# Four output blocks side by side on the column tiles of a modulation product, with transposes in place of selecting sums

## The chip, the cores and the metric

The kernel runs on one NeuronCore of one Trainium2 chip. The metric is device time in microseconds (us) of one execution, lower is better. The five engines (PE, the matrix engine; DVE, the vector engine; ACT, the scalar engine; POOL, the general one; SP, which here issues nearly all DMA loads) run their own instruction streams and wait for each other by semaphores.

## The reference, cut to what matters

One decoder layer over 288 token columns: 256 of a prompt, and 8 sample sequences of 4. Everything is float32. A conditioning vector `c`, one for each of the nine sequences, is multiplied by a large weight matrix to give six modulation vectors of width 2048:

```python
mod = (c @ w_ada + b_ada)[:, None, :]                 # c: 9 x 2048, w_ada: 2048 x 12288
sh1, sc1, gt1, sh2, sc2, gt2 = jnp.split(mod, 6, axis=-1)
h = rmsnorm(x, g_norm1) * (1 + sc1) + sh1
proj = h @ w_in                                       # mixer projections and three gates
branches = jnp.einsum('blnw,nwd->blnd', jnp.stack([y_a, y_b, y_c], axis=2), w_br)
merged = jnp.sum(gate * branches, axis=2)
x = x + gt1 * (merged @ w_o)
h2 = rmsnorm(x, g_norm2) * (1 + sc2) + sh2
x = x + gt2 * hier_moe(h2, ...)
```

`w_ada` is 100.7 MB of the 456 MB that the kernel moves. Its 12288 output columns fall into 24 blocks of 512. Blocks 0 to 3 are `sh1`, 4 to 7 `sc1`, 8 to 23 the other four vectors.

## The kernel before, in words

The program is written by hand, engine by engine, with semaphores; the order of the work is the order of the code. It goes through these stages:

1. **Loading stage.** `x` and `c` arrive, PE sums squares for the norm, and then the first 8 blocks of the modulation product (`sh1`, `sc1`) are computed while their 32 MB stream in through the eight 1 MB slots of `ring8`. As soon as the scales and shifts of a quarter of the model width are known, DVE and ACT modulate that quarter of `xa` and split it into a high part `hh` and a low part `hl`, which float32r products need.
2. **Mix stage.** 48 tiles of 128 output columns of `w_in`, each of two halves, each half 8 x 3 products (lines 1155 to 1157: weights high by x high, high by low, low by high). ACT makes the high part of the weights (`split_hi`, line 595), DVE the low part (`split_lo`, line 765), three buffers deep.
3. **Gates stage.** A loop of 16 steps over `ot`. A step has three gate tiles (six halves), three branch halves, and one of the other 16 modulation blocks, whose weights come through two 1 MB buffers `adaw`.
4. **The `w_o` product**, then routing, 16 experts (a loop over 4 groups), and the output.

**How a modulation block is computed.** The stationary operand is a slice of `cT`: 128 rows (one of the 16 slices `kt` of the contraction) by 32 columns, of which 9 are sequences. It fills a quarter of the PE array's columns, so four such products run side by side on the four column tiles, each writing 32 partitions of PSUM bank 6. Before, `ada_chunk` (line 1126) gives the four column tiles four *different slices of the contraction* of the *same* block: bank 6 ends with four partial sums in partitions 0, 32, 64 and 96. So a block is closed by a selecting sum: ACT copies bank 6 to `part` (`save_part`, line 604), and `ada_select` (line 1135) multiplies each 128 columns of `part` by `sel`, a 0/1 matrix of 9 columns used here, which adds the four partial sums and turns the block so that model width lies on partitions. DVE then adds the bias (`save_mod`) and writes `mod`. All this happens once for every block, 24 times.

In the loading stage a block's 4 chunks `j` are used one by one as they land: PE waits for one slot, does 4 products, and increments `ada_used`; SP waits on `ada_used` to load the slot again (line 309), and the first mixer weights `mixw` (line 315), which lie over the same slots, wait on it too. The blocks come in the order 0, 4, 1, 5, 2, 6, 3, 7, so that each pair completes one quarter `q`. DVE does for each `q`: two `save_mod`, `scales` (line 797), `modulate` (lines 765, 811), a wait for ACT's `hh`, and `hl`. ACT does for each `q`: two `save_part`, its half of `modulate` (line 610), and `hh` (line 623). Only after the fourth quarter do they split the first mixer weights.

In the gates stage PE does the block's chunks 0 and 1 after the first gate tile and 2 and 3 after the third, and `ada_select` after the second branch half.

## Time and profile before

| what | value |
|---|---|
| device time, median of 3 runs | 1684.76 us (1684.45 to 1692.87) |
| profiled execution: span from first to last instruction | 1679.3 us |
| profiled execution: its own device time | not given apart; the fastest run is 5.15 us above the span |
| PE busy | 1587.3 us, 95% of the span |
| DVE, ACT, POOL busy | 41%, 29%, 14% |
| granted PE clock, mean | 0.967 of full |
| DMA | 456.46 MB, 272 GB/s mean |

The profile is one execution on the chip. A line number names a line of the kernel; a helper's line (765 is DVE's `tt`) stands for all its callers, so DVE rows are told apart by the tiles. A float32 product of the modulation, of the selecting sums or of a transpose shows as two MATMUL records, a float32r product (lines 1155 to 1157) as one. A matmul's printed duration includes its way through the pipeline, so the pace of a stream is read from the distances between starts.

### The profile page before, as it was taken

The numbers are of one execution on the slowest core, as the hardware profiler recorded it, in microseconds if no ns is written. First come the engines' busy times: TensorE is split into PE (matmuls) and PEld (weight loads), VectorE is DVE, ScalarE is ACT, GpSimd is POOL, SyncE is SP. The second block draws the span as 40 slices with busy tenths as digits, with TensorE's granted clock in tenths as the row PEclk, the third lists the DMA queues.
The fourth block names the chain that finished last, engine by engine and source line by source line (L and its number), as shares of the span: only waits on it lengthen the run. The fifth ranks groups of instructions, "written<-read, shape, count | busy, mean of one in ns | idle before, by whom it ended". The sixth has DMA issues, their size and how long they took to land.

```text
span 1679.3 us, 27852 instructions
## 1 busy us (share of the span) xinstructions
PE 1587.3 (95%) x10634; PEld 1199.8 (71%) x10634; DVE 686.4 (41%) x1368; ACT 482.7 (29%) x613; POOL 235.2 (14%) x368
## 2 busy tenths in 40 slices
PE   5779999999999999999999989969999999999995
PEld 2169999999899898989898989945345345345342
DVE  2134444434434333434343345572342443443446
ACT  2133333334334433443344333240101101101102
POOL 0017678603200000000000002220000000000002
PEclk9689999999999999999999999977999999999996
DMA  9994545441565676567666765243998998998991
GB/s 379 422 370 165 178 161 177 158 171 58 209 277 236 252 295 273 241 245 298 271 247 240 299 267 175 78 173 135 410 421 361 407 422 361 411 422 356 409 384 56
DMA packets 63102, 456.46 MB, mean 272 GB/s; under 512 B 7728, under 2 KB 8112, under 8 KB 9440
## 3 DMA queue, kind: packets, MB, share of 16 engines
q1 hardware_dynamic: 62352, 454.66, 68.3%
q0 software_dynamic: 720, 1.41, 0.2%
q8 instruction: 17, 0.28, 0.1%
q14 instruction: 13, 0.11, 0.0%
HBM read 452.93 MB, written 3.12 MB: 272 GB/s over the span
## 4 chain that ended last, share of the span: by engine, by line
PE 89%; DMA 5%; DVE 4%; ACT 1%; issue 1%; SPq 0%; POOL 0%; DVEq 0%; ACTq 0%
PE bank L1155 18%; PE bank L1156 17%; PE bank L1157 17%; PE bank L1357 13%; PE bank L1395 7%; DMA ring<-in_w_ada 5%; PE bank L1126 4%; PE bank L1328 3%; PE bank L1313 2%; PE bank L1330 1%; PE bank L1379 1%; PE bank L1135 1%; PE bank L1385 1%; PE bank L1413 1%; PE bank L1345 0%
## 5 line engine op out<-in xcount | busy, mean ns | idle before, releaser
L765 DVE TENSOR_TENSOR wl<-mixw,wh 128x1024 fp32r<-128x1024 f32 x224 | 288.4, 1289 | 460.8 <-ACT wh L595 454.1
L1155 PE MATMUL bank<-hh,wh 128*128 128x288 f32 x1536 | 458.1, 298 | 8.1 <-DVE wl L765 6.7
L1156 PE MATMUL bank<-hl,wh 128*128 128x288 f32 x1536 | 454.3, 296 | 0.0
L1157 PE MATMUL bank<-hh,wl 128*128 128x288 f32 x1536 | 452.6, 295 | 0.0
L595 ACT ACTIVATE wh<-mixw 128x1024 fp32r<-128x1024 f32 x224 | 236.8, 1058 | 345.9 <-PE bank L1157 340.9
L1155 PEld LDWEIGHTS bank<-hh,wh 128*128 128x128 f32 x1536 | 288.8, 188 | 21.8 <-issue 14.9
L1157 PEld LDWEIGHTS bank<-hh,wl 128*128 128x128 f32 x1536 | 290.1, 189 | 0.0
L1156 PEld LDWEIGHTS bank<-hl,wh 128*128 128x128 f32 x1536 | 289.2, 188 | 0.1
L1359 PE MATMUL bank<-ring,xg 128*64 128x512 f32 x512 | 232.0, 600 | 0.0
L1357 PE MATMUL bank<-ring,xg 128*64 128x512 f32 x512 | 232.0, 600 | 0.0
L1357 PEld LDWEIGHTS bank<-ring,xg 128*64 128x64 f32 x512 | 67.3, 138 | 132.1 <-issue 131.6
L1395 PE MATMUL bank<-dring,hid 128*64 128x512 f32 x512 | 113.4, 595 | 13.3 <-DVE hid L765 13.3
L1039 DVE SCALAR_TENSOR_TENSOR x<-bank,mod,x 128x256 f32<-128x256 f32 x272 | 118.1, 477 | 0.0
L1155 PE MATMUL bank<-ysp,wh 128*128 128x288 f32 x384 | 116.4, 303 | 0.0
L1156 PE MATMUL bank<-ysp,wh 128*128 128x288 f32 x384 | 113.1, 294 | 0.0
L1157 PE MATMUL bank<-ysp,wl 128*128 128x288 f32 x384 | 112.7, 293 | 0.0
L765 DVE TENSOR_TENSOR wl<-brw,wh 128x1024 fp32r<-128x1024 f32 x48 | 58.8, 1225 | 99.4 <-ACT wh L595 99.4
L765 DVE TENSOR_TENSOR scaled<-bank,mod 128x32 f32<-128x32 f32 x272 | 38.9, 185 | 144.8 <-PE bank L1313 144.8
L1395 PEld LDWEIGHTS bank<-dring,hid 128*64 128x64 f32 x512 | 35.3, 137 | 81.0 <-issue 64.0
L1155 PE MATMUL bank<-mh,wh 128*128 128x288 f32 x256 | 77.2, 302 | 5.3 <-DVE ml L765 5.3
L1155 PEld LDWEIGHTS bank<-ysp,wh 128*128 128x128 f32 x384 | 72.1, 188 | 13.4 <-issue 13.4
L576 POOL TENSOR_TENSOR sq<-sq 128x288 f32<-128x288 f32 x8 | 6.6, 827 | 533.1 <-ACT sq L753 533.1
(229 smaller groups left out, 1938.3 us busy)
## 6 DMA issues: line engine op xcount, KB each, us to landing
adaw<-in_w_ada SPq DMA_DIRECT2D x64, 1024.0 KB, 5.9
ring<-in_w_gate SPq DMA_DIRECT2D x64, 1024.0 KB, 10.9
ring<-in_w_up SPq DMA_DIRECT2D x64, 1024.0 KB, 12.8
dring<-in_w_down SPq DMA_DIRECT2D x64, 1024.0 KB, 12.8
mixw<-in_w_mix SPq DMA_DIRECT2D x48, 1024.0 KB, 5.0
mixw<-in_w_gt SPq DMA_DIRECT2D x48, 1024.0 KB, 8.5
ring<-in_w_ada SPq DMA_DIRECT2D x32, 1024.0 KB, 17.8
brw<-in_w_br SPq DMA_DIRECT2D x16, 1536.0 KB, 9.4
```

Source lines behind the costliest of these rows:

```text
L595: act.activation(wh[:, b], src, ACT.Copy).then_inc(hi_ready, 1)
L765: return dve.tensor_tensor(out, a, b, op)
L1039: dve.scalar_tensor_tensor(x1[:, f, 0:TP], bank[b + h][:, 0:TP], mod[:, GT2 + f, 0:1], x1[:, f, 0:TP], ALU.mult, ALU.add)
L1126: last = mm(bank[6][32 * q:32 * q + 32, :], cT[:, 4 * j + q, :], buf[:, q, :], start=j == 0, stop=j == ADA_CHUNKS - 1, tile_position=(0, 3 ...
L1155: mm(out, wh[:, s, k, :], hi[:, first + k, :], start=start and k == 0, stop=False)
L1156: mm(out, wh[:, s, k, :], lo[:, first + k, :], start=False, stop=False)
L1157: last = mm(out, wl[:, s, k, :], hi[:, first + k, :], start=False, stop=stop and k == HALF - 1)
L1313: last = mm(bank[b + h][:, 0:T], y[rows, P * j:P * j + P], sT[e_before % 2][rows, :], start=part_ == 0, stop=part_ == 1, tile_position=(64 ...
L1328: mm(bank[b][:, 256 * d:256 * d + 256], thi[0:n, t_, f0:f0 + P], oh[0:n, t_, :], start=t_ == 0, stop=False)
L1357: a = mm(bank[0][0:CAP, :], xg[:, kt, slots], gate[:, k, :], start=kt == 0, stop=kt == KT - 1, tile_position=(0, 0))
L1359: b = mm(bank[0][CAP:2 * CAP, :], xg[:, kt, slots], up[:, k, :], start=kt == 0, stop=kt == KT - 1, tile_position=(0, CAP))
L1395: last = mm(bank[2 + b][CAP * h:CAP * h + CAP, :], hid[:, c, :], dring[k][:, 1024 * h + 512 * b:1024 * h + 512 * b + 512], start=c == 0, s ...
```

## The change

Each column tile now holds its own output block, and the contraction runs over time: all four tiles use the same slice `kt` of `cT` and different weights. After 64 products bank 6 holds four finished blocks, in partitions 0, 32, 64 and 96. A set of four blocks is closed at once: ACT copies bank 6 as before, `ada_select` multiplies each 128 columns of `part` by the identity (128 columns in place of 9), which is a transpose, and DVE picks four groups of 9 columns out of bank 7 with one addition for each block. There are 6 closings in place of 24.

In the loading stage the 8 blocks are 2 sets (blocks 0, 4, 1, 5, and 2, 6, 3, 7). A group of 16 products needs four slots, and all four are released at its end. Closings come after the 4th and the 8th group of four chunks. In the gates stage a set takes four steps, with 16 products in each as before; the closing stands in the fourth. The loop of the gates stage is now 4 iterations of 4 steps on PE, 3 of 4 and then 4 single ones on ACT and DVE, and is written out on SP. A load into `adaw` now gathers four pieces of 2 KB per partition, where it was one of 8 KB.

```diff
-ADA1_BLOCKS = 8
+ADA_SETS = 2
@@ SP, loading stage
-            for k in range(8):
-                sp.dma_start(ring8[k][:], ada_src(slice(4 * (k // 4), 4 * (k // 4) + 1), k % 4))\
-                    .then_inc(slot_loaded[k], 16)
-            with sp.Fori(0, 3) as it:
-                for k in range(8):
-                    sp.wait_ge(ada_used, it * 8 + (k + 1))
-                    sp.dma_start(ring8[k][:], ada_src(ds(it + (1 + 4 * (k // 4)), 1), k % 4))\
-                        .then_inc(slot_loaded[k], 16)
+            for c in range(ADA_SETS * 16):
+                n, j, g = c // 16, c // 4 % 4, c % 4
+                if c >= 8:
+                    sp.wait_ge(ada_used, c - 7)
+                sp.dma_start(ring8[c % 8][:], w_ada[2 * n + g // 2 + 4 * (g % 2), j]).then_inc(slot_loaded[c % 8], 16)
@@ SP, gates stage
-                sp.dma_start(adaw[j % 2][:], ada_src(ds(ot + ADA1_BLOCKS, 1), j))\
+                b0 = 4 * (ADA_SETS + ot // 4)
+                sp.dma_start(adaw[j % 2][:], w_ada[b0:b0 + 4, ot % 4, :, j, :].rearrange("g p n -> p g n"))\
                     .then_inc(ada_loaded[j % 2], 16)
-            with sp.Fori(0, KT - 1) as ot:
+            for ot in range(KT - 1):
@@ ACT
             def save_part(n):
-                act.wait_ge(ada_used, n * 4 + 4)
+                act.wait_ge(ada_used, n * 16 + 16)
...
             for q in range(4):
-                save_part(2 * q)
-                save_part(2 * q + 1)
+                if q % 2 == 0:
+                    save_part(q // 2)
                 modulate(xa, a1, SH1, q, q + 1)
@@ DVE
+            picked = bank[7].rearrange("p (c g s) -> p g c s", g=4, s=32)[:, :, :, 0:NSEQ]
+            def save_mod_pair(n):
+                dve.wait_ge(ada_sel, n + 1 + 1)
+                for a, first in enumerate((SH1, SC1)):
+                    for h in range(2):
+                        to = slice(first + 8 * n + 4 * h, first + 8 * n + 4 * h + 4)
+                        last = tt(mod[:, to, :], picked[:, 2 * h + a], par[:, to].unsqueeze(2).broadcast_to([P, 4, NSEQ]), ALU.add)
+                last.then_inc(mod_ready, 1)
...
             for q in range(4):
-                save_mod(2 * q, SH1 + 4 * q)
-                save_mod(2 * q + 1, SC1 + 4 * q)
-                dve.wait_ge(mod_ready, 2 * q + 3)
+                if q % 2 == 0:
+                    save_mod_pair(q // 2)
+                    dve.wait_ge(mod_ready, q // 2 + 2)
                 scales(a1, SC1, C_G1, 4 * q, 4)
@@ PE
+            def ada_row(g, kt, weights):
+                return mm(bank[6][32 * g:32 * g + 32, :], cT[:, kt, :], weights, start=kt == 0, stop=kt == KT - 1,
+                          tile_position=(0, 32 * g))
             def ada_select(n):
...
-                    last = mm(bank[7][:, NSEQ * c:NSEQ * c + NSEQ], part[:, P * c:P * c + P], sel[:, 0:NSEQ], start=True, stop=True)
+                    last = mm(bank[7][:, P * c:P * c + P], part[:, P * c:P * c + P], ident[:], start=True, stop=True)
...
+            for n in range(ADA_SETS):
+                pe.wait_ge(part_ready, n + 1)
+                for j in range(ADA_CHUNKS):
+                    for g in range(4):
+                        pe.wait_ge(slot_loaded[4 * (j % 2) + g], 16 * (2 * n + j // 2 + 1))
+                    for k in range(4):
+                        done = [ada_row(g, 4 * j + k, ring8[4 * (j % 2) + g][:, k, :]) for g in range(4)]
+                    for last in done:
+                        last.then_inc(ada_used, 1)
+                ada_select(n)
...
+            def gates_step(m, i):
+                ot = m * 4 + i
...
-                    if n == 1:
-                        ada_select(ot + ADA1_BLOCKS)
+                    if n == 1 and i == 3:
+                        ada_select(m + ADA_SETS)
```

How the instructions move, at three places. `bank` is PSUM, `ring` a slot of `ring8`, `a_142` the scales, and the number behind x is how often a row stands in a run.

PE in the loading stage before, one of four iterations of a loop over two blocks:

```order
L1126 MATMUL bank<-ring_49,cT 32x512 x4
L1126 MATMUL bank<-ring_50,cT 32x512 x4
L1126 MATMUL bank<-ring_51,cT 32x512 x4
L1126 MATMUL bank<-ring_52,cT 32x512 x4
L1132 REGISTER_ALU
L1135 MATMUL bank<-sel,part 128x9 x4
L1126 MATMUL bank<-ring_53,cT 32x512 x4
```

and after the change, the end of a set:

```order
L1136 MATMUL bank<-ring_53,cT 32x512
L1136 MATMUL bank<-ring_54,cT 32x512
L1136 MATMUL bank<-ring_55,cT 32x512
L1136 MATMUL bank<-ring_56,cT 32x512
L1144 MATMUL bank<-ident,part 128x128 x4
```

Products that used one slot four times now go around four slots, and the closing comes after 64 products, not after 16.

DVE in the loading stage before, the last two quarters and the first splits of mixer weights:

```order
L765 TENSOR_TENSOR mod<-bank,par 128x36 x2
L797 SCALAR_TENSOR_TENSOR a_142<-mod,par 128x36
L765 TENSOR_TENSOR xa<-xa,a_142 128x4x32
L811 TENSOR_SCALAR xa<-xa,a_142,mod 128x256 x2
L765 TENSOR_TENSOR xa<-xa,mod 128x4x32
L765 TENSOR_TENSOR hl<-xa,hh 128x1152
L765 TENSOR_TENSOR wl<-mixw_61,wh 128x1024 x2
```

and now:

```order
L761 TENSOR_TENSOR mod<-bank,par 128x36 x4
L805 SCALAR_TENSOR_TENSOR a_142<-mod,par 128x36
L761 TENSOR_TENSOR xa<-xa,a_142 128x4x32
L819 TENSOR_SCALAR xa<-xa,a_142,mod 128x256 x2
L761 TENSOR_TENSOR xa<-xa,mod 128x4x32
L761 TENSOR_TENSOR hl<-xa,hh 128x1152
L805 SCALAR_TENSOR_TENSOR a_142<-mod,par 128x36
L761 TENSOR_TENSOR xa<-xa,a_142 128x4x32
L819 TENSOR_SCALAR xa<-xa,a_142,mod 128x256 x2
L761 TENSOR_TENSOR xa<-xa,mod 128x4x32
L761 TENSOR_TENSOR hl<-xa,hh 128x1152
L761 TENSOR_TENSOR wl<-mixw_61,wh 128x1024 x2
```

Two quarters now stand behind one closing, where each quarter had its own.

PE in the gates stage before, between the second and the third branch half of every step:

```order
L1155 MATMUL bank<-ysp,wh 128x288
L1156 MATMUL bank<-ysp,wh 128x288
L1157 MATMUL bank<-ysp,wl 128x288
L1132 REGISTER_ALU
L1135 MATMUL bank<-sel,part 128x9 x4
L1152 REGISTER_ALU
```

and at the same place of the first three steps of four now:

```order
L1167 MATMUL bank<-ysp,wh 128x288
L1168 MATMUL bank<-ysp,wh 128x288
L1169 MATMUL bank<-ysp,wl 128x288
L1164 REGISTER_ALU
L1167 MATMUL bank<-ysp,wh 128x288
```

The four closing products are gone from three steps of four.

## Rows read from the trace of the kernel before

**Rows 1.** Span of the core, and its mean granted clock

```profile
core 0: 1679.3 us, clock 0.967
```

**Rows 2.** Stages: length, busy time by engine (instructions), granted clock, DMA share, GB/s

```profile
102.00:440.00 338.00, 334.66 (x2452) 329.96 (x2453) 146.17 (x139) 126.01 (x159) 183.07 (x290) 0.99 0.47 161
440.00:975.00 535.00, 535.00 (x4066) 483.72 (x4065) 206.21 (x233) 211.77 (x236) 2.31 (x4) 1.00 0.67 267
```

**Rows 3.** Chain that ended last: start, us, what; loading stage, one of four stretches

```profile
74.34 18.59 DMA ring<-in_w_ada
```

**Rows 4.** Timeline, loading stage: start, us, engine, line; what ended its idle time

```profile
22.14 3.64 PE L1126 MATMUL bank<-ring,cT 128*32 128x512 f32 x32
...
80.54 1.85 PE L1126 MATMUL bank<-ring,cT 128*32 128x512 f32 x8 [0.56 <-DMA ring<-in_w_ada]
```

**Rows 5.** Timeline, end of the loading stage, engines mixed

```profile
90.48 1.07 PE L1126 MATMUL bank<-ring,cT 128*32 128x512 f32 x8 [0.95 <-DMA ring<-in_w_ada]
...
92.97 1.06 PE L1126 MATMUL bank<-ring,cT 128*32 128x512 f32 x8 [1.42 <-DMA ring<-in_w_ada]
...
94.10 0.60 ACT L604 ACTIVATE part<-bank 128x512 f32<-128x512 f32 x1 [9.35 <-PE bank L1126]
...
94.75 1.06 PE L1135 MATMUL bank<-sel,part 128*128 128x9 f32 x8 [0.72 <-ACT part L604]
95.85 0.20 DVE L765 TENSOR_TENSOR mod<-bank,par 128x36 f32<-128x36 f32 x1 [9.61 <-PE bank L1135]
96.08 0.20 DVE L797 SCALAR_TENSOR_TENSOR a<-mod,par 128x36 f32<-128x36 f32 x1
...
99.92 1.36 DVE L765 TENSOR_TENSOR hl<-xa,hh 128x1152 fp32r<-128x1152 f32 x1 [2.35 <-ACT hh L623]
...
102.47 0.61 PE L1155 MATMUL bank<-hh,wh 128*128 128x288 f32 x1 [6.66 <-DVE wl L765]
```

**Rows 6.** Windows of 2 us after PE's start at 102.47: columns as in Rows 2

```profile
104.00:106.00 2.00, 2.00 (x11) 2.00 (x10) 0.69 (x1) 0.00 (x0) 0.00 (x0) 0.50 1.01 420
106.00:108.00 2.00, 2.00 (x16) 2.00 (x16) 0.00 (x0) 0.44 (x1) 0.00 (x0) 0.98 1.00 400
```

**Rows 7.** Chain that ended last, gates stage

```profile
460.97 1.85 PE bank L1126 x16
...
469.35 0.79 PE bank L1135 x8
```

**Rows 8.** PE timeline around one closing of the gates stage

```profile
469.05 0.30 PE L1157 MATMUL bank<-ysp,wl 128*128 128x288 f32 x1
469.18 0.96 PE L1135 MATMUL bank<-sel,part 128*128 128x9 f32 x8
469.99 0.38 PE L1155 MATMUL bank<-ysp,wh 128*128 128x288 f32 x1
470.21 0.29 PE L1156 MATMUL bank<-ysp,wh 128*128 128x288 f32 x1
```

**Rows 9.** Timeline of one expert: four 128 by 128 products with the identity, and what follows

```profile
1174.87 1.16 PE L1385 MATMUL bank<-ident,gus 128*128 128x128 f32 x8
...
1175.96 0.41 PE L1313 MATMUL bank<-sT,yhi 64*128 64x288 f32 x2
```

**Rows 10.** Loads into `adaw`: time to landing

```profile
DMA to landing us min/median/max: 4.8/5.9/8.2
```

**Rows 11.** SP's queue, gates stage: one pair of loads into `adaw`

```profile
447.35 1.17 SPq L347 DMA_DIRECT2D adaw<-in_w_ada  x2
```

**Rows 12.** Waits of PE's weight loads in the gates stage: us in total, times, longest

```profile
PEld bank L1155 <- issue: 26.8, 32, 0.8
...
PEld bank L1126 <- DMA adaw<-in_w_ada: 0.6, 1, 0.6
```

**Rows 13.** Instruction pages over the whole span: packets, MB, share

```profile
q8 instruction: 17, 0.28, 0.1%
```

**Rows 14.** PE's weight loads on leaving the loop over the experts

```profile
1648.00 0.20 PEld L1313 LDWEIGHTS bank<-sT,yhi 64*128 64x128 f32 x2 [2.97 <-issue]
```

More of the change, by code:

```diff
@@ L674, in gates_step @@
                     split_hi(unit(ot, 2 * n + 4))
-                save_part(ot + ADA1_BLOCKS)
+                if closed is not None:
+                    save_part(closed + ADA_SETS)
                 for k in (9, 10, 11):
                     split_hi(unit(ot, k))
-            with act.Fori(0, KT - 1) as ot:
-                gates_step(ot, gate_unit)
-            gates_step(KT - 1, gates_then_wo)
+            with act.Fori(0, KT // 4 - 1) as m:
+                for k in range(4):
+                    gates_step(m * 4 + k, gate_unit, m if k == 3 else None)
+            for ot in range(KT - 4, KT - 1):
+                gates_step(ot, gate_unit, None)
+            gates_step(KT - 1, gates_then_wo, KT // 4 - 1)
             for q in range(3):
@@ L886, in gates_step @@
                 tt(dst, dst, gt[:, 0, :], ALU.add).then_inc(merged_ready, 1)
-            with dve.Fori(0, KT - 1) as ot:
-                chain.loop(ot, 3)
-                gates_step(ot, gate_unit)
-            chain.end(KT - 1)
-            gates_step(KT - 1, gates_then_wo)
+            with dve.Fori(0, KT // 4 - 1) as m:
+                chain.loop(m, 12)
+                for k in range(4):
+                    gates_step(m * 4 + k, gate_unit, m if k == 3 else None)
+            chain.end(KT // 4 - 1)
+            for ot in range(KT - 4, KT - 1):
+                gates_step(ot, gate_unit, None)
+            gates_step(KT - 1, gates_then_wo, KT // 4 - 1)
             merged_rests(3)
@@ L1120, in _ @@
             sums.quarter = 0
-            def ada_chunk(buf, j, loaded, value):
-                pe.wait_ge(loaded, value)
-                for q in range(4):
-                    last = mm(bank[6][32 * q:32 * q + 32, :], cT[:, 4 * j + q, :], buf[:, q, :], start=j == 0,
-                              stop=j == ADA_CHUNKS - 1, tile_position=(0, 32 * q))
-                last.then_inc(ada_used, 1)
+            def ada_row(g, kt, weights):
+                return mm(bank[6][32 * g:32 * g + 32, :], cT[:, kt, :], weights, start=kt == 0, stop=kt == KT - 1,
+                          tile_position=(0, 32 * g))
             def ada_select(n):
@@ L1225, in branch, with ada_rows @@
                 half(gate_unit(ot, 6 + n), 3 + n, hi, lo, 0, True, True)
-            def gates_step(ot):
+            def ada_rows(ot, i, j):
+                pe.wait_ge(ada_loaded[j % 2], ot * 32 + (16 if j < 2 else 32))
+                for g in range(4):
+                    last = ada_row(g, 4 * i + j, adaw[j % 2][:, g, :])
+                last.then_inc(ada_used, 1)
+            def gates_step(m, i):
+                ot = m * 4 + i
                 for n in range(3):
@@ L1239, in gates_step @@
                     branch(ot, n)
-                    if n == 1:
-                        ada_select(ot + ADA1_BLOCKS)
+                    if n == 1 and i == 3:
+                        ada_select(m + ADA_SETS)
             pe.wait_ge(yc_ready, WT)
-            with pe.Fori(0, KT) as ot:
-                gates_step(ot)
+            with pe.Fori(0, KT // 4) as m:
+                for i in range(4):
+                    gates_step(m, i)
             with pe.Fori(0, 5) as v:
```

44 lines of the change are left out of this document (19 added, 25 removed).

## The prediction

> **What bounds the kernel now.** I read the span and clock first [rows 1]: one core, 1679.3 us, clock 0.967, so nearly everything at full speed. Then the busy time by stage [rows 2]: from 102 to 440 us PE works 334.66 of 338 us, from 440 to 975 us all 535 us, with DMA at 0.47 and 0.67. These two stages cost what PE's stream costs. The chain that ended last shows the other kind of stage: before 93 us it runs through DMA in four stretches like the one at 74.34 us [rows 3], and PE only comes in for a few products where each chunk lands. The timeline shows how that stage ends [rows 5]: the last chunk is used at 92.97 us, then ACT copies, PE closes the block, DVE and ACT modulate the last quarter, and PE starts the mix stage at 102.47 us. From there on PE's work is one chain, so whatever the end of the loading stage gains or loses goes into the time in full. In the gates stage the chain shows the modulation's products (1.85 us for 8) and its closing (0.79 us) in PE's own path [rows 7]. So the change has two prices with nothing between them: the tail of the loading stage, where latency counts, and the gates stage, where PE's busy time counts. The other six closings of the loading stage lie under DMA and are worth nothing.
>
> **What the gates stage gains.** Around one closing, PE's starts are 469.05, 469.18, 469.99 and 470.21 [rows 8]. The stream's pace is 0.13. Without the closing the fourth start would be at 469.31, so a closing costs 0.90 us, with its re-entry. Sixteen of them cost 14.4 us. Afterwards there are four, of 128 columns each. Their nearest row is four products of the same 128 by 128 weights with the identity in the expert stage: 1174.87 to 1175.96, or 1.09 us [rows 9], against 0.81 here (469.18 to 469.99). So one costs 0.90 + 0.28 = 1.18 us, four 4.7 us. **Gain 9.7 us**; between 9.0 (a closing of 1.35 us, if reading or writing is slower at this place) and 10.8 (no dearer than before). The products themselves stay 16 per step at the same pace.
>
> What else moves there costs nothing, with these covers. ACT's and DVE's closing work (0.60 and 0.20 us) leaves three steps and DVE's becomes 4 x 0.20 us in the fourth; PE waits for neither, as it is 100% busy. The loads into `adaw` become pieces of 2 KB; they landed in 4.8 to 8.2 us [rows 10], and a pair issued at 447.35 [rows 11] is used at 460.97 [rows 7], after 13.6 us, so they may take half as long again before PE notices. Only the very first pair had no slack: PE waited 0.6 us for it once [rows 12]; should it land late by as much as its slowest landing, 8.2 us, is above the fastest, 4.8, that is 3.4 us, once. I take zero and keep 3.4 for the range. SP issues the same loads behind the same counts, since `ada_used` still rises by 4 a step.
>
> **What the tail of the loading stage loses.** Four steps, from the landing of the last chunk at 92.97 us.
>
> First, the products. Before, the last chunk needed 4 products, 94.10 - 92.97 = 1.13 us. Now PE waits for all four slots of the last group and does 16 products behind the last landing. Sixteen at full clock took 3.64 us, four at half clock 1.85 us, so 7.4 us for sixteen [rows 4]. Between the groups PE is idle: four chunks land in 4 x 2.49 = 9.96 us (92.97 - 90.48 is the pace [rows 5]), so a burst of 3.6 to 7.4 us is followed by 2.6 to 6.3 us of nothing. How such a burst runs is shown by PE's start of the mix stage: after some 6.7 us of waiting it goes at 0.50 (1.2 GHz) until 106 us and at 0.98 (nearly 2.4 GHz) after it [rows 6], so for 3.6 us. A burst that starts like this does 3.6 / 7.4 = 49% of its work at half clock and the rest in 1.85 us: 5.45 us. Against it stands that PE's last chunks, after waits of about 1.4 us, ran at full clock [rows 5]; by that row it would be 3.64 us. I take 5.45, as the wait is nearer to the 6.7 us than to the 1.4. Loss 4.3 us (2.5 to 6.3).
> The Trainium skill, TensorE: Matmul & The Clock Gate, in the section on HAM oscillation, describes a loop whose short bursts between waits for DMA each start at the low clock. By that rule the first step loses the 4.3 us, and without it 2.5; the row of the mix stage's start agrees with the rule, the row of the last chunks does not.
>
> Second, ACT's copy is the same 0.60 us, and the closing has 128 columns: + 0.28 us, as above. Third, DVE does 4 additions where one lay on the path (0.20 us each, 95.85 to 96.08 is their pace): + 0.7 us. Fourth, and largest: two quarters are now modulated behind the last closing. A quarter is a chain that hands over four times (DVE scales, modulates; ACT modulates, makes `hh`; DVE makes `hl`), and DVE's order lets no second quarter start before the first's `hl`. It runs from 96.08 to 99.92 + 1.36 = 101.28: **+ 5.2 us**. The bounds are narrow, as the work is the same. **Loss 4.3 + 0.3 + 0.7 + 5.2 = 10.5 us**, 8.7 to 12.5.
>
> The mixer weights are not late: four of six can load as soon as the seventh group is done, and would be in before 103 us; PE now starts at 113.
>
> Is DMA still kept busy? Slots now come free four at a time. With a burst of 5.45 us the next four loads are issued 4.5 us before DMA runs dry, with a fully slow burst of 7.4 us only 2.6 us before. What a load needs until its data flow is bounded by the fastest landing, 4.8 us [rows 10], less the 2.49 us of its own transfer: 2.3 us. So it is covered, barely in the worst case. I take zero.
>
> **The sum.** + 10.5 - 9.7 = + 0.8 us on a span of 1679.3, so 1680.1 us. The profiled execution's own time is not given; the three runs lie 5.15 us and more above the span, the median 5.5 us. I add the difference to the median: 1684.76 + 0.8 = **1685.6 us**, no change. The sum's bounds are 8.7 - 10.8 = - 2.1 and 12.5 + 3.4 - 9.0 = + 6.9 us. A measurement of this kernel tells about 0.5%, 8.4 us, from no change, and both bounds lie inside it.
>
> **Rivals.**
> *Code pages at the loop's end: slower.* PE's loop of the gates stage grows fourfold, to some 2,070 instructions (2,000 for the products, the rest registers and branches). The longest loop that PE ran before is that over the experts, some 1,440. Over the whole span 17 pages of 16 KB came [rows 13], while PE's loops went round 7, 16, 5 and 4 times; 0.28 MB is 63 bytes for each of the 4,460 instructions of PE's program, so each seems to have come once and loops of up to 1,440 to stay resident; of 2,070 no row tells. If it does not, each of three jumps back waits for a page. In the old gates loop no jump shows: the longest idle time put to issue is 0.8 us [rows 12]. The nearest row of PE leaving a loop is 2.97 us put to issue [rows 14]; three such are + 8.9 us, which gives 1694.5 us. Above 2.5 us a jump the change is slower than no change by over 0.5%. For it: the size. Against it: PE's instructions are issued ahead of the array, which hides part of a fetch. Chance 0.12.
> The Trainium skill, Runtime: NRT & Kernel Launch, in the section on instruction fetch mechanics, gives PE's instruction memory 2,048 instructions and says that a taken branch to a page outside it has to fetch it before going on. By that rule this rival happens; no run so far shows the limit.
>
> *DMA runs dry between groups: slower.* Six times four slots are freed late. Were the issue to data time 2.3 us plus SP's own issue of 0.5 us a load, and bursts slow throughout, each boundary would lose some 0.5 to 2 us: + 3 to + 12 us, 1689 to 1698 us. For it: the margin is small. Against it: the pace of landings has never depended on PE, and a burst of 5.45 us leaves 2 us. It decides above 1.3 us a boundary. Chance 0.06.
>
> *The tail is shorter: faster.* If bursts run at full clock and closings were free in both stages, the change would be + 8.7 - 14.4 = - 5.7 us, 1679.1 us. That is still within 0.5%. For more, something in PE's stream must run faster than before, perhaps as four tiles now share one slice of `cT`; but the moving operands, which differ before and after alike, set the 1.85 us for 8 products, and the slices of `cT` load in parallel to them; no row shows time that such sharing would free. Chance of over 0.5% faster: 0.04.
>
> **How the numbers follow.** My own case has 0.78, the code pages 0.12, dry DMA 0.06, faster 0.04. Of the two slower rivals about half of the chance lies above 8.4 us; I add some for a cost that I have not seen, since the gain is read from rows at one place and the loss hangs on a chain. Faster 0.05, same 0.80, slower 0.15. The range goes from the sum's lower bound with a little for the spread of runs, 1681, to the code pages' time without their last microsecond, 1693.5.
>
> **What the new profile would show.** Right: PE's start in the mix stage at about 113 us; 16 products after the last landing, near 93 us, in 5 to 6 us; two chains of 5.2 us behind it; a gates stage about 9.7 us shorter, with four closings of 1.1 us; DMA above 0.97 until 93 us; the rest only shifted. Wrong: instruction packets on q8 well above 25 and a gap on PE every 132 us (the code pages); a last landing after 94 us (dry DMA); waits of PE for `adaw` in more than the first step (the 2 KB pieces); a start of the mix stage before 110 us (the tail).

## The result, and the profile after

The change takes 1718.47 us (median of 4 runs, 1716.75 to 1723.32) beside 1684.61 us for the kernel before (4 runs, 1684.25 to 1692.87): **slower by 2.0%, ratio 1.0197 with the interval 1.0169 to 1.0224**. I had forecast 1685.6 us and a range up to 1693.5, so it lies 25 us above the range. The profiled execution is the slowest of the four (1723.32 us); the spans of the other three are 1716.4, 1715.0 and 1717.1 us.

Span and clock first, against [rows 1]:

```profile
core 0: 1721.6 us, clock 0.950
```

Then the stages, against [rows 2]: windows with length, busy time by engine (instructions), granted clock, DMA share, GB/s. The rows are most of the loading stage, the mix stage, two stretches ahead of the gates stage, and the gates stage.

```profile
20.00:90.00 70.00, 40.07 (x236) 11.69 (x234) 14.72 (x22) 5.55 (x8) 0.00 (x0) 0.73 1.00 407
115.00:440.00 325.00, 324.73 (x2382) 321.77 (x2383) 136.12 (x113) 122.81 (x155) 175.09 (x277) 0.99 0.45 156
442.00:450.00 8.00, 6.52 (x29) 5.25 (x26) 4.75 (x12) 1.64 (x2) 3.03 (x6) 0.68 0.00 0
450.00:458.00 8.00, 6.77 (x24) 5.54 (x24) 4.90 (x15) 0.00 (x0) 5.58 (x10) 0.50 0.01 2
458.00:1025.00 567.00, 539.43 (x4000) 484.74 (x4000) 211.77 (x237) 178.96 (x204) 1.11 (x2) 0.98 0.78 255
```

PE is now idle for 567.00 - 539.43 = 27.6 us of the gates stage, and its clock is no longer 1.00. Of the idle time 5.3 us were there before too, the wait for `ml` at the stage's end; the other 22.3 us are new. This is the loss. The stage's edges are two starts of PE, here before the change:

```profile
439.47 0.39 PE L1155 MATMUL bank<-hh,wh 128*128 128x288 f32 x1 [1.39 <-DVE proj L765]
...
984.20 0.60 PE L1155 MATMUL bank<-mh,wh 128*128 128x288 f32 x1 [5.28 <-DVE ml L765]
```

and after it:

```profile
458.21 0.60 PE L1167 MATMUL bank<-hh,wh 128*128 128x288 f32 x1 [1.44 <-DVE proj L761]
...
1025.21 0.60 PE L1167 MATMUL bank<-mh,wh 128*128 128x288 f32 x1 [5.26 <-DVE ml L761]
```

The 42.3 us between the two spans lie in four places:

| stretch | before | after | difference |
|---|---|---|---|
| to PE's start of the mix stage | 102.47 | 115.27 | + 12.8 |
| from there to the first product of the gates stage | 337.00 | 342.94 | + 5.9 |
| gates stage, to the first product with `mh` | 544.73 | 567.00 | + 22.3 |
| the rest | 695.1 | 696.4 | + 1.3 |

The second line is the half clock of the windows from 442 to 458 (0.68 and 0.50; before it was 1.00 at this place). It begins behind an idle time of 1.5 us that PE has at this place in every kernel profiled, and it is not the change's: with the loading stage of the kernel before, three of the nine experiments below show it too (342.6 to 342.9 us in the second row) and six do not (337.2 to 337.8). Without it the profiled execution would be about where the other three are. Where it occurs it also runs on into the gates stage, at 0.50 for the first 4 to 5 us, and costs some 2 us there; this bears on the comparisons below.

**The gates stage.** Waits, with us in total, times, longest; for PE and for its weight loads (PEld):

```profile
PE bank L1167 <- issue: 18.4, 3, 6.3
...
PE bank L1136 <- DMA adaw<-in_w_ada: 3.7, 6, 1.8
...
PEld bank L1136 <- DMA adaw<-in_w_ada: 12.6, 12, 2.7
```

Three waits of 5.9 to 6.3 us for nothing that the profile shows; and the wait for `adaw`, once 0.6 us before [rows 12], is there a dozen times. The loads into `adaw` land in twice the time of [rows 10]:

```profile
DMA to landing us min/median/max: 7.4/11.8/14.5
```

One of the three gaps in PE's timeline, and the clock behind it (windows as above):

```profile
594.22 0.29 PE L1169 MATMUL bank<-ysp,wl 128*128 128x288 f32 x1
...
600.80 0.60 PE L1167 MATMUL bank<-hh,wh 128*128 128x288 f32 x1 [6.29 <-issue]
```
```profile
602.00:604.00 2.00, 2.00 (x10) 2.00 (x10) 0.00 (x0) 0.00 (x0) 0.00 (x0) 0.50 0.00 0
606.00:608.00 2.00, 2.00 (x17) 2.00 (x17) 0.61 (x1) 1.06 (x1) 0.00 (x0) 1.00 0.00 0
```

The gap stands between the last product of one turn of PE's loop and the first of the next. PE was idle for 6.29 us and then works at 0.50, half speed (1.2 GHz), for some microseconds, as at its start of the mix stage [rows 6]. The page says what was fetched meanwhile; before it was 17 packets [rows 13]:

```profile
DMA packets 87720, 457.12 MB, mean 266 GB/s; under 512 B 7728, under 2 KB 8112, under 8 KB 42208
...
q8 instruction: 55, 0.90, 0.2%
```

Right behind the gap the chain that ended last leaves PE:

```profile
609.46 1.90 PE bank L1136 x16
611.37 14.23 DMA adaw<-in_w_ada
625.64 1.06 PE bank L1136 x8
```

**The tail of the loading stage**, timeline, against [rows 5]:

```profile
95.11 6.12 PE L1136 MATMUL bank<-ring,cT 128*32 128x512 f32 x32 [4.56 <-DMA ring<-in_w_ada]
...
101.37 0.60 ACT L596 ACTIVATE part<-bank 128x512 f32<-128x512 f32 x1 [29.73 <-PE bank L1136]
...
102.02 1.16 PE L1144 MATMUL bank<-ident,part 128*128 128x128 f32 x8 [0.79 <-ACT part L596]
103.22 0.50 DVE L761 TENSOR_TENSOR mod<-bank,par 128x36 f32<-128x36 f32 x4 [30.18 <-PE bank L1144]
103.75 0.20 DVE L805 SCALAR_TENSOR_TENSOR a<-mod,par 128x36 f32<-128x36 f32 x1
...
107.60 1.36 DVE L761 TENSOR_TENSOR hl<-xa,hh 128x1152 fp32r<-128x1152 f32 x1 [2.35 <-ACT hh L615]
108.88 0.19 DVE L805 SCALAR_TENSOR_TENSOR a<-mod,par 128x36 f32<-128x36 f32 x1
...
115.27 0.61 PE L1167 MATMUL bank<-hh,wh 128*128 128x288 f32 x1 [12.09 <-DVE wl L761]
```

The last landing is at 95.11 (before 92.97): 2.1 us later. The 16 products behind it take 101.37 - 95.11 = 6.26 us, where the last chunk took 1.13: + 5.1. The closing takes 1.20 (1.10): + 0.1. The four additions take 0.53 (0.23): + 0.3. The second quarter takes 108.88 - 103.75 = + 5.1. Together 12.7 of the 12.8 us. The 2.1 us vary from profile to profile: the last landing is at 92.97 to 93.80 us in the kernels with the loading stage of before and at 93.63 to 95.90 in the seven with the new one, 1.8 us apart in the medians, and PE's starts of the mix stage are 12.0 us apart in the medians (103.1 and 115.1).

### The profile page after: what moved, and what is told of

It reads as the page before. It is cut to its first block, busy times and chain, and to the rows that moved or that the text cites. A ratio compares the mean times of both kernels' runs of the same rounds, so it can differ in the third digit from the quotient of the medians.

```text
span 1721.6 us, 26797 instructions
## 1 busy us (share of the span) xinstructions
PE 1584.8 (92%) x10490; PEld 1199.9 (70%) x10490; DVE 685.7 (40%) x1368; ACT 441.1 (26%) x571; POOL 234.7 (14%) x368
## 4 chain that ended last, share of the span: by engine, by line
PE 82%; DMA 11%; DVE 4%; ACT 2%; issue 1%; SPq 1%; POOL 0%; DVEq 0%; ACTq 0%
PE bank L1167 15%; PE bank L1169 15%; PE bank L1168 15%; PE bank L1379 13%; PE bank L1417 7%; DMA adaw<-in_w_ada 6%; PE bank L1136 5%; DMA ring<-in_w_ada 4%; PE bank L1350 3%; PE bank L1335 2%; PE bank L1352 1%; PE bank L1401 1%; PE bank L1407 1%; DMA x<-in_x 1%; PE bank L1229 1%
## 5 line engine op out<-in xcount | busy, mean ns | idle before, releaser
L1167 PEld LDWEIGHTS bank<-hh,wh 128*128 128x128 f32 x1536 | 292.7, 191 | 46.5 <-issue 34.1
L1169 PEld LDWEIGHTS bank<-hh,wl 128*128 128x128 f32 x1536 | 293.6, 191 | 0.0
L1168 PEld LDWEIGHTS bank<-hl,wh 128*128 128x128 f32 x1536 | 293.0, 191 | 0.1
## 6 DMA issues: line engine op xcount, KB each, us to landing
adaw<-in_w_ada SPq DMA_DIRECT2D x64, 1024.0 KB, 11.8
ring<-in_w_up SPq DMA_DIRECT2D x64, 1024.0 KB, 12.8
dring<-in_w_down SPq DMA_DIRECT2D x64, 1024.0 KB, 12.8
```

The costliest lines, as they stand in the source:

```text
L1167: mm(out, wh[:, s, k, :], hi[:, first + k, :], start=start and k == 0, stop=False)
L1168: mm(out, wh[:, s, k, :], lo[:, first + k, :], start=False, stop=False)
L1169: last = mm(out, wl[:, s, k, :], hi[:, first + k, :], start=False, stop=stop and k == HALF - 1)
```

## The experiments

Two suspects in the gates stage, PE's loop of four steps and the loads in pieces, and one in the loading stage. My theory after the result: **the loop's code no longer stays resident, and the pieces, far apart in memory, make the loads and the fetches slow**. Rivals: the size of the pieces (2 KB); the pieces alone, the gaps being a consequence of them; the 128-column closings. Unless said otherwise a kernel is the one before ("B") with one edit; "the change" is the changed kernel. All are compared with B by the ratio of device times and its 95% interval, from several executions; lengths of stages, waits and landings are those of one profiled execution each.

### The loop and the pieces, each alone

**loop4**: B with PE's loop of the gates stage over four steps a turn.

```
-with pe.Fori(0, KT) as ot:
-    gates_step(ot)
+with pe.Fori(0, KT // 4) as m:
+    for i in range(4):
+        gates_step(m * 4 + i)
```

> The kernel before, with one edit: PE's loop of the gates stage has four steps in its body and 4 iterations, as in the change. Same products, same closings, same loads; ACT, DVE and SP untouched. Theory 'code pages': a body of some 2,070 instructions does not stay resident, so each of the three jumps back leaves PE idle for about 6 us (the change showed 18.4 us put to issue, in 3 places), plus some 2.4 us for the stretch at half clock behind it: 15 to 26 us slower than before, near 1700 to 1710, and some 50 instruction packets on q8 instead of 17. Rival 'jumps of ACT and DVE, or the wait for the modulation's weights': nothing here, 1684 to 1686, q8 at about 25.

**loop3**: three steps a turn, the sixteenth behind the loop (`Fori(0, KT // 3)`, three steps, then `gates_step(KT - 1)`).

> The kernel before, with PE's loop of the gates stage written as 5 iterations of three steps and one single step behind. The body is some 1,590 instructions, a little over the longest loop that stayed resident before (1,440). If only a body above about 2,048 is fetched again: no change, 1684 to 1686, q8 about 22. If the limit is lower: four jumps of 6 to 8 us, 1708 to 1717, q8 above 40.

**flat16**: no loop (`for ot in range(KT): gates_step(ot)`).

> The kernel before, with PE's sixteen steps of the gates stage written out, without a loop: some 8,300 instructions in one line. Theory 'the jump back to a page that is gone' costs: no jump, no gap, 1684 to 1686, with about 48 instruction packets on q8. Rival 'fetching itself is too slow or collides with the loads': gaps spread over the stage, more than 10 us slower.

**pieces_far**: the loads into `adaw` in four pieces of 2 KB a partition, 4 MB apart, as in the change; SP's loop of the gates stage is written out for it, here and in pieces_near.

```
+w_ada2[ot // 4, :, ot % 4, :, j, :].rearrange("k p n -> p k n")
```

> The kernel before, with the loads into adaw alone changed: the array of the last 16 blocks is laid out so that a load gathers four pieces of 2 KB per partition, 4 MB apart, with 8 KB from partition to partition, the addresses of the change; SP's gates loop is written out as in the change. Theory 'pieces': landing rises from 5.9 to about 12 us and PE waits some 2 us for the third chunk in every second step: 10 to 18 us slower, 1695 to 1703. Rival 'hidden, as forecast': PE had 13.6 us, the waits in the change came from its other parts: within 3 us of before.

**pieces_near**: the same four pieces of 2 KB, 256 KB apart, and neighbouring partitions 2 KB apart (8 KB in pieces_far).

```
+w_ada2[ot, j].rearrange("k p n -> p k n")
```

> As pieces_far, but the four pieces of 2 KB lie 256 KB apart, and 2 KB from partition to partition, in place of 4 MB and 8 KB. If the size of a piece makes a load slow: landing near 11 us and some 12 us slower than before, like pieces_far. If the places read do: landing back to 6 to 7 us and no loss.

Measured, with the length of the gates stage, the waits of PE put to issue (total, longest), the packets of code on q8, and the median time to landing of `adaw`:

| kernel | ratio (interval) | gates, us | issue | q8 | landing |
|---|---|---|---|---|---|
| B | 1 | 544.73 | none | 17 | 5.9 |
| loop3 | 0.9982 (0.9954 to 1.0011) | 546.79 | none | 24 | 5.7 |
| flat16 | 1.0011 (0.999 to 1.0033) | 544.72 | none | 48 | 6.2 |
| loop4 | 1.0044 (1.0013 to 1.0074) | 552.18 | 5.2, 2.0 | 54 | 5.8 |
| pieces_near | 0.9993 (0.9966 to 1.0021) | 545.84 | none | 17 | 6.5 |
| pieces_far | 1.0059 (1.003 to 1.0088) | 555.90 | none | 17 | 10.9 |

loop3's 2.1 us above B are the half clock ahead of the gates stage, which its profile has and which lasts until 452 us there. loop4's three gaps, its code packets and loop3's, one line each from the waits and the pages:

```profile
PE bank L1155 <- issue: 5.2, 3, 2.0
```
```profile
q8 instruction: 54, 0.88, 0.2%
```
```profile
q8 instruction: 24, 0.39, 0.1%
```

A loop of three steps, some 1,590 instructions with what stands between them, brings 7 packets more than B, about its longer code; one of four, some 2,070, brings 37 more, and a gap at each of its three jumps back. Written out, the same number of instructions comes once and in order (48 packets), and no gap shows. So it is not the number of pages that costs but **the jump to a page that is gone**. Alone the three cost 7.45 us: 5.2 of gaps (1.6, 1.6 and 2.0), and 1.7 as the clock falls to 0.50 for some 3 us, which happens behind the last of them only. I had expected gaps of about 6 us and 15 to 26 us in all, so the loop alone is not the change's loss:

```profile
850.49 0.40 PE L1155 MATMUL bank<-hh,wh 128*128 128x288 f32 x1 [1.97 <-issue]
851.00:854.00 3.00, 3.00 (x16) 3.00 (x14) 0.80 (x2) 0.00 (x0) 0.00 (x0) 0.52 0.00 0
```

That the pages fetched again are those of this loop is read from the count of packets and from where the gaps stand; the profile shows no single fetch.
The Trainium skill, Runtime: NRT & Kernel Launch, in the section on instruction fetch mechanics, gives PE's instruction memory as 2,048 instructions; a limit between 1,590 and 2,070 agrees with it.

The pieces alone cost 11.2 us when they lie far apart and 1.1 us, 0.9 of it in one wait of the first step, when they lie near. **Their size is hardly it, their places are**: both kernels move the same 87679 packets. The time to landing, and PE's waits in pieces_far, from its tile and wait views:

```profile
DMA to landing us min/median/max: 7.4/10.9/14.7
PE bank L1128 <- DMA adaw<-in_w_ada: 7.7, 8, 4.1
```

and in pieces_near:

```profile
DMA to landing us min/median/max: 5.0/6.5/9.4
```

The median landing of 10.9 us is still below the 13.6 us from issue to use in B, but the slowest, 14.7, is not. More than half of the waiting stands in the very first step, whose loads were issued at 439.79, only 8.4 us before PE came to them:

```profile
448.20 1.06 PE L1128 MATMUL bank<-adaw,cT 128*32 128x512 f32 x8 [0.25 <-DMA adaw<-in_w_ada]
453.38 1.93 PE L1128 MATMUL bank<-adaw,cT 128*32 128x512 f32 x8 [4.11 <-DMA adaw<-in_w_ada]
```

These 4.4 us, and the half clock behind them (0.50 until after 456 us, 1.6 us lost), are 6.0 of the 11.2. The other six waits are 0.2 to 0.9 us each, with the clock at 1.00 behind them.
The Trainium skill, DMA: Bandwidth & Descriptors, in the section on latency and other measured facts, tells of copies whose row pitch is a large power of two: 103 GB/s at 4 MiB where 207 were had at 512 KiB, with the clash of channels as an inference. There the pitch is from partition to partition, here it is between the four pieces within one, so the rule is only akin; that near and far places differ agrees with it. pieces_near differs from pieces_far in three ways at once: pieces 256 KB apart and not 4 MB, partitions 2 KB apart and not 8, and so a load that reads 1 MB in one run and not 2 KB of every 8. Which of them counts no run here shows.

### Both together

**loop4_pieces**: B with the edits of loop4 and pieces_far. **loop4_near**: B with those of loop4 and pieces_near. **pieces_flat**: B with far pieces and PE's steps written out.

> The kernel before with both edits at once: PE's loop body of four steps (alone 1.0044 of before, some 8 us) and adaw loads in four pieces of 2 KB, 4 MB apart (alone 1.0059, some 10 us). If the two add up: 16 to 21 us slower than before, gaps at the jumps of 2 us. Theory 'they multiply': in the change a jump left PE idle for 6.3 us, in loop4 for 2.0, in the change with 8 KB pieces 2.3, as instruction pages come through DMA engines that are busy with small packets: here gaps near 6 us and 26 to 34 us slower.

> The kernel before with PE's loop body of four steps and the near pieces of 2 KB. With the far pieces the same loop was 1.020 of before, where the two alone gave 1.0044 and 1.0059, and its three gaps were 16.4 us against 5.2. Theory 'far places': here as loop4 alone, 1.003 to 1.006, gaps near 5 us in all. If packets in number do it: above 1.012.

> The kernel before with the far pieces of 2 KB and PE's steps written out. On the change written out (a_flat) the far pieces cost the gates stage only 1.7 us (537.8 against 536.1 us for 8 KB pieces), on the kernel before in a loop of one step 11.2 us (555.9 against 544.7). If the loop form matters (each step's waits or its jump come later than in straight code): 1 to 4 us slower than before, waits for adaw short. If the order of the products within a step or chance decides: 8 to 12 us slower, as pieces_far.

| kernel | ratio (interval) | gates, us | over B |
|---|---|---|---|
| loop4_pieces | 1.02 (1.017 to 1.0231) | 579.53 | + 34.8 |
| loop4_near | 1.0059 (1.003 to 1.0088) | 555.94 | + 11.2 |
| pieces_flat | 1.0017 (0.9993 to 1.0041) | 548.89 | + 4.2 |

PE's waits in loop4_pieces, in loop4_near and in pieces_flat, a fence each:

```profile
PE bank L1157 <- issue: 16.4, 3, 6.8
PE bank L1128 <- DMA adaw<-in_w_ada: 8.5, 8, 3.0
```
```profile
PE bank L1157 <- issue: 4.5, 2, 2.3
```
```profile
PE bank L1128 <- DMA adaw<-in_w_ada: 1.0, 3, 0.5
```

The two edits are dearer together than apart: 34.8 us, where 7.45 + 11.2 = 18.7 were due; by the ratios 2.0% against 0.44% + 0.59%. The three gaps grow from 5.2 to 16.4 us (3.8, 6.8 and 5.8) with far pieces, and to 7.0 with near ones: 4.5 put to issue, and a third of 2.5 at the same product of the loop, which the profile puts to `wl` on DVE. These two edits alone reproduce the loss of the change, 1.02 beside 1.0197, with nothing of its closings or its loading stage, which nearly cancel there (below). That the gaps are 3.8 to 6.8 us instead of 1.6 to 2.0 when far pieces are in flight is measured; that the fetch queues behind them in the DMA engines is my reading of it.

pieces_flat's 4.2 us are not all the pieces'. Its profile has the half clock ahead of the gates stage, and it runs on until 451 us: 2.4 of the 4.2 us. This also brought PE to its first `adaw` only 9.8 us after the issue, and the wait of 4.4 us of pieces_far's first step is not there. What remains for the pieces is 1.8 us in this profile against the 5.2 that pieces_far has outside its first step; by the ratios, 1.0017 against 1.0059, writing the steps out helps, but the intervals overlap.

### The change with one thing undone

**a_8k**: the change, `w_ada` laid out so that a load is one run of 8 KB a partition. **a_near**: pieces of 2 KB, 256 KB apart. **a_flat**: pieces as in the change, PE's steps written out. **a_8k_flat**: a_8k and a_flat together. ACT's and DVE's loops stay as in the change in all four.

```
a_8k     +sp.dma_start(adaw[j % 2][:], w_ada2[ot, j])
a_near   +w_ada2[ot, j].rearrange("g p n -> p g n")
a_flat   +for ot in range(KT): gates_step(ot // 4, ot % 4)
```

> The change, with one edit: the weights of the last 16 blocks are laid out so that a load into adaw is one piece of 8 KB per partition again. Theory 'pieces': landing back to 6 us, no wait of PE for them, and the three gaps at the loop's end shrink from 6.3 us to the 1.7 us that loop4 showed, since pages no longer queue behind small packets: 18 to 24 us faster than the change, so 8 to 14 us slower than before. Rival 'the gaps at the loop's end are long for another reason': 10 to 13 us faster than the change, gaps still near 6 us.

> The change, with the weights of the last 16 blocks laid out so that the four pieces of 2 KB of a load lie 256 KB apart and 2 KB from partition to partition; still four pieces, still PE's loop. pieces_near showed on the kernel before that such pieces land in 6.5 us and cost nothing, pieces_far that those 4 MB apart land in 10.9 us. Theory 'the places, not the size': as the change with 8 KB pieces (1694, 1.0057 of before), gaps at the jumps near 2 us. Theory 'number of packets delays the instruction pages': gaps near 6 us, 1708 to 1718.

> The change, with PE's sixteen steps written out and nothing else. The pieces of 2 KB stay. If the jumps cost the change 3 x (6.3 us of gap + 2 to 3 us at half clock behind it): 18 to 27 us faster than the change, so 8 to 15 us slower than before. If pieces stall a page anywhere, not only at a jump: less than 10 us faster than the change, with gaps put to issue spread over the stage.

> The change with 8 KB pieces and without PE's loop: what is left of it is the tail of the loading stage and the four closings. By loading_only (1.0079, +11 to 13 us) and the mixture (0.992, -12 us): within 3 us of before. It is what the change was forecast to do with neither of the two costs that were taken as zero.

| kernel | loop | pieces | ratio (interval) | gates, us |
|---|---|---|---|---|
| the change | 4 x 4 | far | 1.0197 (1.0169 to 1.0224) | 567.00 |
| a_near | 4 x 4 | near | 1.0081 (1.0051 to 1.0111) | 547.47 |
| a_8k | 4 x 4 | 8 KB | 1.0057 (1.0027 to 1.0086) | 545.70 |
| a_flat | out | far | 1.0023 (1.0004 to 1.0043) | 537.80 |
| a_8k_flat | out | 8 KB | 0.9995 (0.9965 to 1.0026) | 536.07 |

Waits of a_8k, with its third gap from the timeline, and of a_flat:

```profile
PE bank L1166 <- issue: 4.0, 2, 2.3
587.34 0.60 PE L1166 MATMUL bank<-hh,wh 128*128 128x288 f32 x1 [2.52 <-DVE wl L760]
```
```profile
PE bank L1136 <- DMA adaw<-in_w_ada: 0.8, 1, 0.8
```

The table is the accounting of the gates stage. Without both suspects it takes 536.07 us, 8.7 less than B. The loop of four steps with loads of 8 KB puts 9.6 on it (545.70), far pieces on top 21.3 (567.00), but only 1.7 on the steps written out (537.80). - 8.7 + 9.6 + 21.3 = + 22.2 of the 22.3 us. a_near's gaps stand at the same three products, 2.6 to 3.0 us each, all put to `wl`.

The clock at the stage's start has to be taken off. The profiles of the change, a_flat and a_8k_flat begin the gates stage at half clock, those of B, a_8k and a_near do not. The same start in the kernel "best" of the next section, with B's below it:

```profile
446.00:448.00 2.00, 2.00 (x9) 2.00 (x10) 0.00 (x0) 0.00 (x0) 0.95 (x2) 0.50 0.77 319
448.00:450.00 2.00, 2.00 (x11) 2.00 (x10) 0.00 (x0) 0.00 (x0) 0.00 (x0) 0.50 1.00 422
```
```profile
440.00:442.00 2.00, 2.00 (x17) 2.00 (x17) 0.00 (x0) 0.00 (x0) 1.84 (x4) 1.00 0.98 414
```

PE starts 9 and 11 products in 2 us, where B starts 17. Summed over windows of 1 us, this takes 2.3 us from a_8k_flat, 2.1 from a_flat and 1.9 from the change. Without it the closings gain 10.9 us (idle time and half clock taken off, B's stage is 539.45 us and a_8k_flat's 528.50), about twelve times the 0.90 us of one closing; the loop costs 11.9 (6.5 in its three gaps, 5.0 at half clock behind them), more than in B; and far pieces on top cost 19.4. **With PE's steps written out the change costs 0.2%, and with loads of 8 KB as well nothing that can be measured, as forecast; the two gates suspects together make it 2%.**
That the closings are not to blame shows in PE's timeline of the change, around one of them, against [rows 8]:

```profile
590.13 0.30 PE L1169 MATMUL bank<-ysp,wl 128*128 128x288 f32 x1
590.26 1.06 PE L1144 MATMUL bank<-ident,part 128*128 128x128 f32 x8
591.08 0.38 PE L1167 MATMUL bank<-ysp,wh 128*128 128x288 f32 x1
591.29 0.30 PE L1168 MATMUL bank<-ysp,wh 128*128 128x288 f32 x1
```

From 590.13 to 591.29 is 1.16; less two steps of the pace, 0.26, that is 0.90 us, as for the nine columns before.

### The loading stage, and the best mixture

**loading_only**: B with the change's loading stage (two sets of 16 chunks, a closing of 128 columns each). **loading_contig**: the same, and the blocks lie in memory in the order in which they are loaded (`w_ada1[n, j, g]`), which tells places from the order of freeing.

> The kernel before with the loading stage of the change alone: two sets of four blocks, closed by transposes, two quarters behind each closing. The gates stage is that of before (16 closings by selecting sums). The change's trace has PE's start of the mix stage at 115.27 us against 102.47: 2.1 us from a later last landing, 5.1 from sixteen products behind it instead of four, 5.2 from the second quarter, the rest from the closing. Theory 'the tail adds in full': 11 to 14 us slower. Rival 'part of it is taken up later, where something else waits': under 8 us slower.

> As loading_only, but the first 8 blocks are laid out in memory in the order in which they are loaded, so that four loads in a row read 4 MB in one piece instead of from four blocks 1 MB and 4 MB apart. If the later last landing (95.1 against 93.0 us; 405 GB/s against 422) comes from the places read: landing back near 93 us, 2 us faster than loading_only. If it comes from slots that are released four at a time: as loading_only within 0.5 us.

loading_only: 1.0079 (1.0052 to 1.0107), PE in the mix stage at 114.61, gates stage 544.71. loading_contig: 1.0064 (1.0044 to 1.0083), 115.72, last landing 95.74. Their windows from 20 to 90 us, loading_only first, columns as above:

```profile
20.00:90.00 70.00, 39.81 (x241) 12.41 (x239) 14.72 (x22) 5.56 (x8) 0.00 (x0) 0.78 1.01 412
```
```profile
20.00:90.00 70.00, 38.78 (x232) 11.46 (x234) 14.72 (x22) 5.55 (x8) 0.00 (x0) 0.76 1.00 406
```

and B in the same window:

```profile
20.00:90.00 70.00, 53.52 (x306) 15.19 (x304) 18.46 (x31) 11.38 (x17) 0.00 (x0) 0.76 1.01 422
```

B moves 422 GB/s, the change 407. With the blocks in order it is no better, so the later last landing does not come from places. Slots being freed four at a time are what is left of my two suspects; no run changes that alone. The delay is not a steady one: in the change the groups land 9.9 us apart, as before, except for one boundary of 11.55 us (63.74 to 75.29), and in a_flat, with the same loading stage, no boundary is above 10.2 us (last landing 93.63). All of the tail is lost whatever the gates stage does: 12.1 and 13.2 us here, 11.3 to 12.8 in the versions of the change.

**best**: the loading stage of B, the change's closings in the gates stage, loads of 8 KB, PE's steps written out.

> A mixture: the loading stage of before (8 blocks, selecting sums), the gates stage of the change (4 sets, transposes), its weights in pieces of 8 KB, and PE's sixteen steps written out without a loop. Every cost found so far is gone and the gain of 12 closings is left: by the sum 9.7 us faster than before. If the closings were hidden by something, or sharing a slice of cT costs: under 4 us.

**0.992 (0.9889 to 0.9951)**: 1671.0 us beside 1683.36, the only version that beats the kernel before. The gates stage takes 535.92 us:

```profile
445.00:981.00 536.00, 530.67 (x4000) 479.15 (x4000) 211.95 (x239) 179.00 (x204) 1.53 (x3) 0.99 0.67 270
```

8.8 us less than B's, with none of the tail's loss. This profile too begins the stage at half clock (2.1 us), so the gain is 10.9 us, 0.65%; the rest of the 0.8% is within the interval.

## Why the prediction was wrong

**The step that failed** is the paragraph "What else moves there costs nothing, with these covers": the gates stage was to become 9.7 us shorter and became 22.3 us longer. The loads into `adaw` stand in it with "I take zero and keep 3.4 for the range". I weighed the size of the pieces, and that a landing half as long again would still be covered by 13.6 us. Size costs 1.1 us (pieces_near); their places, which I did not weigh at all though the edit's pattern of addresses shows them, give landings of 10.9 to 11.8 us in the median, twice as long, and 14.7 at worst. In the gates stage that is + 11.2 us on B alone. The 3.4 us was kept for the right place, the very first pair, which in pieces_far costs 4.4 us of waiting and 1.6 of half clock behind it; the other 5.2 us were in no bound. PE's loop is not among the covers at all; it was left to a rival, and the sum had nothing for it.

**The rival that came true** is the code pages, at 0.12. Its mechanism and place are as written: q8 above 25 (55), a gap on PE at each of three jumps. Its price was about right alone: 8.9 us forecast, 7.45 (loop4) and 11.9 (a_8k against a_8k_flat) measured, though as gaps of 1.6 to 2.5 us and the rest at half clock, not as gaps of 2.97. Its chance was too low. What I held against it, that PE's instructions are issued ahead of the array, did not keep the gaps away; how much of a fetch it hides no run shows. The loop's instructions, some 2,070, stood against a limit that the Trainium skill's Runtime: NRT & Kernel Launch, in the section on instruction fetch mechanics, states as 2,048, and no row spoke against the limit. That is more than 0.12.

**What no case had** is that these two multiply. Each of them had its price with the other absent. Loop and pieces together cost the change 30.9 us (567.00 - 536.07) and B 34.8; apart they cost B 18.7. The sum had nothing for either, the range some 8 us above it, and no price had gaps of 6 us.

**The tail** was right in mechanism and 2.3 us too small. 10.5 forecast, 12.8 measured: the products 5.1 (4.3 forecast, 6.26 us for sixteen, between my 5.45 and the 7.4 of a burst wholly at half clock), the second quarter 5.1 (5.2), closing 0.1 (0.3), additions 0.3 (0.7, as all four take 0.50 us together), and 2.1 for the late landing, where I had taken zero. This looks like the rival of the dry DMA in its mildest form: its sign was there, a last landing after 94 us, but it is 2.1 us, 1.6 of them at one boundary, and not 3 to 12. Of the two rules for the burst, that of the Trainium skill's TensorE: Matmul & The Clock Gate, in the section on HAM oscillation (each short burst behind a wait starts at the low clock), was the one to follow here: the trace agrees, with 6.26 us, a burst that starts at 0.50 and has full clock again only after 100 us. It does not hold for every group: the burst at 85.21 us began at full clock, though PE had waited 4.1 us for it, and fell to 0.50 within it.

**The gates gain** was 9.7 forecast. The stage of a_8k_flat is 8.7 us shorter and best's 8.8, below my lower bound of 9.0, but both profiles begin it at half clock. Without that the gain is 10.9 us, at my upper bound of 10.8: one closing costs the same 0.90 us before and after, and the 0.28 us that I added for 128 columns are not there.

**Right by parts**: two chains of 5.1 us behind the last closing, and closings of 1.1 us. a_8k_flat is the kernel that I forecast: + 0.8 us predicted; by its stages 12.6 - 10.9 = + 1.7, without the half clock that its profile has and B's has not; ratio 0.9995 (0.9965 to 1.0026), no change. That two errors of some 1 to 2 us, in the tail and in the gain, cancel in it is luck.

**Open.** How loop and pieces make each other dearer. Why the waits for far pieces outside the first step are longer where B's PE loops over single steps (3.3 us in six) than where the steps are written out (1.0 us in three), though they land as late (7.4 to 14.7 and 6.9 to 14.4 us). Which property of the places makes the pieces late. And why the half clock ahead of the gates stage comes in six of the seventeen profiles.

## What to carry to other kernels

Count an engine's instructions in a loop before unrolling it: here a PE loop of some 1,590 instructions stayed resident and one of 2,070 stopped for a fetch at each jump back, while the same code written out cost nothing; what doesn't fit should be written out or kept to fewer steps.

When a load becomes several pieces, look at where they lie and not only at their size, and lay out the weights so that they lie together. Price two suspects of one stage together as well as apart: here they cost 34.8 us together, 7.45 and 11.2 apart. And before comparing two profiles of a stage, look whether both begin it at the same clock; here that was worth 2 us, as much as some of the effects looked for.

## What was not expected of the hardware

- Four pieces of 2 KB per partition, 4 MB apart and 8 KB from partition to partition, landed in 10.9 us in the median; 256 KB apart and 2 KB from partition to partition in 6.5; one run of 8 KB in 5.9.
- A jump back in a loop of some 2,070 PE instructions left PE idle for 1.6 to 2.5 us with loads of 8 KB (loop4, a_8k), 2.3 to 3.0 with near pieces (loop4_near, a_near) and 3.8 to 6.8 with far ones (the change, loop4_pieces); behind 15 of these 18 gaps PE went on at 0.50 for some 3 to 7 us, even behind one of 1.76 us (a_8k).
- Closing with 128 columns instead of 9 costs PE's stream the same 0.90 us.
- With ring slots freed four at a time the stream ran at 406 to 415 GB/s in all seven kernels, freed one by one at 422 or 423 in all ten, though the DMA share stayed at 1.00.
- A stretch of half clock ahead of the gates stage, worth 5.9 us and some 2 us more within it, comes in six of seventeen profiles, with no edit at that place.
